# Reordering the gate pieces of the attention heads, and the opening's order, in a hybrid diffusion step

## The reference

```python
for l in range(DEPTH):
    ada = silu(c) @ w_ada[l] + b_ada[l]            # 9 vectors of 1024: shift, scale, gate
    h += 0.5 * g0 * swiglu(norm(h), ...)           # D_FF = 2816
    proj = n @ w_in[l]                             # hy, q_a, kv_a, k_r, fn, gates (3 x 1024)
    y_a = hyena(hy, filters(l))                    # two filters, made from a small sine MLP
    p = softmax(q @ k.T * scale); y_b = p @ v      # 8 heads, keys = latent + cached context
    y_c = real(fft2(fn))
    y = (sigmoid(ga)*y_a + sigmoid(gb)*y_b + sigmoid(gc)*y_c) @ w_out[l]
    h += g1 * y
    h += 0.5 * g2 * swiglu(norm(h), ...)
```

## Time and profile before

| | |
|---|---|
| median of three runs | 3245.68 us |
| profiled execution | 3245.85 us, span 3244.1 us |
| TensorE busy (matmul) | 3102.3 us, 96% |
| TensorE weight loads busy | 3025.4 us, 93% |
| VectorE busy | 1743.3 us, 54% |
| ScalarE busy | 966.7 us, 30% |
| mean granted clock of TensorE | 0.982 of full |

### The profile page before, as it was taken

One profiled execution on the slowest core, in us unless ns is written; L12 is line 12 of the kernel. 1 busy time (PEld: TensorE's weight loads), 2 busy tenths in 40 slices (PEclk: granted clock), 3 DMA queues, 4 the chain that ended last, 5 costly groups with the idle time before them and its releaser, 6 DMA issues.

```text
span 3244.1 us, 47824 instructions
## 1 busy us (share of the span) xinstructions
PE 3102.3 (96%) x20540; PEld 3025.4 (93%) x20540; DVE 1743.3 (54%) x2873; ACT 966.7 (30%) x1445; POOL 47.4 (1%) x92
## 2 busy tenths in 40 slices
PE   6899999988999999999999999999899999999998
PEld 3799999987899899999999999998789989999998
DVE  5655666556565565344465466565555545632334
ACT  2332322322444433122233121232244433322222
POOL 0000000000000000000000000000000000000000
PEclk8899999989999999999999999999999999999999
DMA  6145543456222523232223343335712252322221
GB/s 258 73 183 206 227 165 141 163 195 240 74 77 97 192 106 110 92 113 84 106 88 124 124 153 126 144 121 229 276 69 82 73 194 104 116 92 79 78 75 63
DMA packets 78933, 430.61 MB, mean 133 GB/s; under 512 B 8849, under 2 KB 12369, under 8 KB 46722
## 3 DMA queue, kind: packets, MB, share of 16 engines
q1 hardware_dynamic: 58656, 324.56, 27.1%
q0 software_dynamic: 9504, 56.78, 4.6%
q10 hardware_dynamic: 10562, 46.21, 3.6%
HBM read 370.73 MB, written 56.79 MB: 132 GB/s over the span
## 4 chain that ended last, share of the span: by engine, by line
PE 78%; DVE 11%; DMA 4%; ACT 4%; issue 3%; ACTq 0%; DVEq 0%; POOL 0%
PE tile_psum L568 37%; PE tile_psum L575 19%; PE tile_psum L919 4%; PE tile_psum L529 3%; PE tile_psum L494 2%; PE tile_psum L923 2%; PE misc_psum L494 2%; PE tile_psum L775 2%; PE tile_psum L534 1%; DVE wlo L1615 1%; PE tile_psum L703 1%; ACT whi L1160 1%; DMA raw<-in_w_proj 1%; DMA raw<-in_w_mix 1%; DVE h L1771 1%
## 5 line engine op out<-in xcount | busy, mean ns | idle before, releaser
L568 PE MATMUL tile_psum<-n_hi,whi 128*128 128x320 f32 x3264 | 744.3, 309 | 4.2 <-issue 2.2
L568 PE MATMUL tile_psum<-n_lo,whi 128*128 128x320 f32 x3264 | 742.3, 309 | 0.0
L568 PEld LDWEIGHTS tile_psum<-n_hi,whi 128*128 128x128 f32 x3264 | 546.4, 188 | 7.2 <-DVE n_lo L1693 4.6
L1615 DVE TENSOR_TENSOR wlo<-raw,whi 128x2048 fp32r<-128x2048 f32 (+2 forms) x202 | 443.5, 2196 | 193.5 <-ACT whi L1160 191.0
L568 PEld LDWEIGHTS tile_psum<-n_lo,whi 128*128 128x128 f32 x3264 | 546.9, 188 | 0.0
L575 PE MATMUL tile_psum<-n_hi,wlo 128*128 128x320 f32 x3264 | 512.1, 308 | 0.0
L575 PEld LDWEIGHTS tile_psum<-n_hi,wlo 128*128 128x128 f32 x3264 | 486.9, 188 | 0.0
L1160 ACT ACTIVATE whi<-raw 128x2048 fp32r<-128x2048 f32 (+2 forms) x202 | 369.9, 1831 | 373.9 <-DMA raw<-in_w_up 180.4
L568 PE MATMUL tile_psum<-x_hi,whi 128*128 128x320 f32 x1408 | 319.9, 308 | 0.0
L568 PE MATMUL tile_psum<-x_lo,whi 128*128 128x320 f32 x1408 | 319.7, 308 | 0.0
L1827 DVE TENSOR_TENSOR hidden<-gate_act,tile_psum 128x320 f32<-128x320 f32 x176 | 85.6, 487 | 375.3 <-ACT gate_act L1259 374.7
(11 more groups left out here) (285 smaller groups left out, 3601.3 us busy)
## 6 DMA issues: line engine op xcount, KB each, us to landing
raw<-in_w_up SPq DMA_DIRECT2D x88, 1024.0 KB, 4.8
w_ada<-in_w_ada SPq DMA_DIRECT2D x128, 512.0 KB, 5.7
raw<-in_w_down SPq DMA_DIRECT2D x32, 1024.0 KB, 4.8
raw<-in_w_gate SPq DMA_DIRECT2D x24, 1024.0 KB, 4.8
whi<-table_keep SPq DMA_DIRECT2D x20, 1024.0 KB, 4.8
wlo<-table_keep SPq DMA_DIRECT2D x20, 1024.0 KB, 7.4
g_keep<-gate_out POOLq DMA_DIRECT2D x48, 320.0 KB, 2.4
gates<-g_keep POOLq DMA_DIRECT2D x16, 960.0 KB, 6.8
```

Source lines behind the costliest of these rows:

```text
L568: pe.matmul(tps[:, t.s, m, 0:TH], blk(p, m * n + k)[0], (hi, lo)[b][:, k, tok], start=k == 0 and b == 0, stop=False)
L1615: dve.tensor_tensor(wlo[:, r, 0:cols], raw[:, r, 0:cols], whi[:, r, 0:cols].bitcast(F32), ALU.subtract)\
```

## The change

Two order lists are rewritten, one wait is moved, and `turn_signs(1)` is moved.

```diff
@@ head_order
-            order += [("S", n), ("F", 0)]
+            order += [("S", n)]
         if 1 <= n <= 5 * HEADS:
             order.append(("N", n - 1))
         if n >= 2:
-            order += [("T", n - 2)] + [("F", 0)] * (n != 2)
+            order += [("T", n - 2), ("F", 0), ("F", 0)]
...
-    order += [("F", 0)] * 2
+    order += [("F", 0)]
@@ first_order
-    beside = [[[("chain",)], at(0, "max") + [("add", 0)] + ada, ada * 2],
-              [ada * 2, [("add", 1)] + at(1, "max"), ada + [("add", 2)] + ada],
-              [ada * 2, [("add", 3)] + at(2, "max"), ada * 2]]
+    ahead = [[("chain",)] + ada * 2, ada * 4, ada * 4]
+    behind = [at(0, "max") + [("add", 0)], [("add", 1)] + at(1, "max") + [("add", 2)], [("add", 3)] + at(2, "max")]
     for n in range(3):
-        steps += [("square", (0, 1, 3)[n])] + at(n, "filter", 0) + beside[n][0] + taps(n + 1, 0, 2)
-        steps += [("round",)] * (n == 1) + [("small",)] * (n == 2)
-        steps += at(n, "filter", 1) + beside[n][1] + [("square", 2)] * (n == 1) + taps(n + 1, 2, 2)
-        steps += [("round",)] * (n == 2) + at(n, "filter", 4) + at(n, "norms") + beside[n][2] + taps(n + 1, 4, 1) + at(n + 1, "abs")
-    steps += [("sums",)] + at(3, "filter", 0) + ...
+        steps += [("square", (0, 1, 3)[n])] + ahead[n] + at(n, "filter", 0) + taps(n + 1, 0, 2)
+        steps += [("round",)] * (n == 1) + [("small",)] * (n == 2) + at(n, "filter", 1) + [("square", 2)] * (n == 1) + taps(n + 1, 2, 2)
+        steps += [("round",)] * (n == 2) + behind[n] + at(n, "filter", 4) + at(n, "norms") + taps(n + 1, 4, 1) + at(n + 1, "abs")
+    steps += [("sums",)] + ada + at(3, "filter", 0) + ...
@@ first_filter on TensorE
                     if l == o == 0:
                         pe.wait_ge(start_tables, due(start_tables, 32))
-                        pe.wait_ge(small_in, due(small_in, 16))
+                elif (l, o, f) == (0, 0, 4):
+                    pe.wait_ge(small_in, due(small_in, 16))
@@ first_taps on VectorE
                 if (l, o, t) == (1, 0, 0):
+                    turn_signs(1)
                     filter_hidden(1)
@@ first_chain on VectorE
-                turn_signs(1)
                 chain(2)
```

More of the change, by code:

```diff
@@ L199, in at @@
         return [(what, *orders[n], *which)]
-    beside = [[[("chain",)], at(0, "max") + [("add", 0)] + ada, ada * 2],
-              [ada * 2, [("add", 1)] + at(1, "max"), ada + [("add", 2)] + ada],
-              [ada * 2, [("add", 3)] + at(2, "max"), ada * 2]]
+    ahead = [[("chain",)] + ada * 2, ada * 4, ada * 4]
+    behind = [at(0, "max") + [("add", 0)], [("add", 1)] + at(1, "max") + [("add", 2)], [("add", 3)] + at(2, "max")]
     steps = taps(0, 0, 2) + taps(0, 2, 2) + taps(0, 4, 1) + at(0, "abs") + [("turned",)] + ada
     for n in range(3):
-        steps += [("square", (0, 1, 3)[n])] + at(n, "filter", 0) + beside[n][0] + taps(n + 1, 0, 2)
-        steps += [("round",)] * (n == 1) + [("small",)] * (n == 2)
-        steps += at(n, "filter", 1) + beside[n][1] + [("square", 2)] * (n == 1) + taps(n + 1, 2, 2)
-        steps += [("round",)] * (n == 2) + at(n, "filter", 4) + at(n, "norms") + beside[n][2] + taps(n + 1, 4, 1) + at(n + 1, "abs")
-    steps += [("sums",)] + at(3, "filter", 0) + at(3, "max") + [("spread", 0, 4)] + at(3, "filter", 1) + [("spread", 4, KT)]
+        steps += [("square", (0, 1, 3)[n])] + ahead[n] + at(n, "filter", 0) + taps(n + 1, 0, 2)
+        steps += [("round",)] * (n == 1) + [("small",)] * (n == 2) + at(n, "filter", 1) + [("square", 2)] * (n == 1) + taps(n + 1, 2, 2)
+        steps += [("round",)] * (n == 2) + behind[n] + at(n, "filter", 4) + at(n, "norms") + taps(n + 1, 4, 1) + at(n + 1, "abs")
+    steps += [("sums",)] + ada + at(3, "filter", 0) + at(3, "max") + [("spread", 0, 4)] + at(3, "filter", 1) + [("spread", 4, KT)]
     steps += at(3, "filter", 4) + at(3, "norms")
```

## The result

The changed kernel takes 3276.23 us (median of four runs, 3273.43 to 3280.64), the kernel before 3246.1 beside it: a ratio of 1.0093, 95% interval 1.0081 to 1.0105, so 30 us slower. The profiled execution spans 3271.6 us, before 3244.1.

A forecast was written before the change was run, and what follows sets the result against it. TensorE's order was taken to set the time, so new waits lengthen the kernel. Opening -10.8, heads +29.4 and half clock +5 sum to +23.6 on 3245.85: 3269 us, range 3246 to 3288.

The forecast's parts named there:

- Rival B: Opening brings next to nothing (crowded ada loads, filters starting at half clock), heads lose as forecast: 3277 us, chance 0.12.
- the heads' sum: Both heads stages: itemised gains and losses of 14.7 us a layer, +29.4 for two, before the half-clock allowance.
- Clock: Half clock behind the heads' new waits of about 2.5 us: +5 us, between 0 and 17.
- The opening: Opening: two long waits move behind ready work, so the first normalisation and FFN start earlier: -10.8 us, between -14 and -7.
- the clock's term: Opening: 1.1 us taken off the earlier start of abs, 11.9 us, for stretches at half clock.
- V0: Start of the heads stage: F5 and F6 come behind T0, idle time ahead of V0 grows to 6.5 us: +2.5 a layer.
- P0, P2 and V1: Heads: T follows P0 and P2 sooner, +0.9 each; at V1 T11 finds tile 0 full, +1.5 a layer.
- V2 and V3: Heads: panel parts delay tile 0, waits of 1.5 and 2.7 us at T21 and T22, likewise V3: +8.3 a layer.
- The new heads: At Q2, Q4 and Q6: delayed maximum, L9 and L13 delay the key's low part, old waits go: +3.2 a layer.
- The end: End of the heads stage: with two fills between T's the waits of 1.78 and 0.80 go: -2.6 a layer.
- an ordinary step: Heads: S, T, F, F instead of S, F, T, F, about 5.0 us a step, slack 1.4: gains and loses nothing.
- Rival A: Heads order costs nothing, if ScalarE gets T20's high part out before R10 matters: 3232 us, not slower, chance 0.15.

The follow-up runs named there:

- heads_only: The kernel before with the three changed lines of the head order alone, its opening untouched: 3279.8 us, ratio 1.0105 to before.
- opening_only: The changed kernel with the three head-order lines as before, so only the opening is changed: 3244.7 us, ratio 0.9998 to before.
- opening_warm2: opening_only plus idle matmuls nobody reads, 3, 4 and 6 ahead of the first three filters' norms, 4 ahead of layer 1's first taps: 3239.9 us, 0.9984.
- after_v0: The changed kernel with gate pieces F5 and F6 back ahead of V0, one fewer behind T4 and T24, panel parts shifting along: 3260.0 us, 1.0044.
- after_panels_late: The changed kernel with every panel part (R, L) that stands between scores and transposes moved behind that step's transposes: 3266.6 us, ratio 1.0064.
- after_v0_alone: The changed kernel with only F5 and F6 back ahead of V0, every other entry keeping its place: 3272.4 us, ratio 1.0083.
- opening_warm: opening_only plus idle matmuls nobody reads, 4, 8 and 8 ahead of the first three filters' norms, 12 ahead of layer 1's first taps: 3243.6 us, 0.9995.

## Why the prediction was right, and where not

It said 3269 and slower; it came to 3276.2, inside the range, slower by 30 and not 23.6 us. Rival B (the opening brings next to nothing, the heads lose as forecast: 3277) describes the outcome better than the forecast, though not by its reasons: VectorE shows no wait for an ada load, and the half clock that cost something fell on the norms and last taps. That the heads' sum fits is partly luck: `heads_only` measured +34.4, the forecast's 29.4 + 5, out of two errors of opposite sign (under Clock, below).

- **The opening, -10.8: mis-sized.** `opening_only` measured -0.7 us, within -3.6 to +2.3. The chain through VectorE was right: with the norms and last taps at full clock (`opening_warm2`) abs began at 98.41 and the first normalisation at 106.84, at the times forecast, and the FFN 12.1 us earlier than before. In part that is luck: the third filter began at 75.71 there, 2.4 us ahead of the 78.1 laid out, and its round took as much longer. The step that failed is the clock's term, "I take off 1.1 for stretches at half clock", with the 2.4, 2.9 and 3.9 us for norms and last taps. From the norms' start to the next filter's first piece (the third time to abs) the forecast has 4.1, 4.6 and 3.9 us, where the addition on VectorE is counted in the first two; the changed kernel took 6.5, 6.5 and 6.8. That is 7.2 of the 8.2 us by which abs came late (106.60 against 98.4). A wait moved ahead of the norms puts the half clock on the norms and the last taps, for which VectorE waits three times in a row. The Trainium skill (TensorE: Matmul & The Clock Gate, Part 1) has the half rate follow idling and full rate return after sustained work; the trace agrees: the windows above have 0.50 to 0.51 behind each of the four waits, and the piece at 89.48, between two of the stretches, is back at 3.62 us.
- **V0, +2.5: right in its wait** (6.5 forecast, 6.50 measured), short in its price. P0 came 3.21 us later into the stage with one piece fewer ahead of it, so 4.97 at equal pieces. The excess fits the half clock, 13.65 us that begin 4.8 us before the wait ends.
- **P0, P2 and V1** (0.9, 0.9, 1.5): right. The waits of T5, T15 and T11 are 0.78, 0.78 and 1.25.
- **V2 and V3, +4.2 each**: T21 and T22 wait 1.29 and 2.14, not 1.5 and 2.7. With half clock the stretches from P3 to P4 and P5 to P6 are 5.3 and 3.8 us longer. The order on the engines (R10 ahead of T20's high part, L11 ahead of T21's low part) is in the rows. But the two waits don't belong one to each part. With R10 and L10 earlier T22's wait is gone, even where L11 still stands ahead of T21's low part (`after_v0`), and T21's 1.24 stays. With R10 and L11 moved behind T20 and T21 (`after_panels_late`) T21's wait is gone and T22's is 1.76.
- **The new heads, +3.2**: S20 and S30 wait 2.13 and 2.12 behind L9 and L13, as written out. T9's 2.4 was 0.67. Unforeseen are T8, T18 and T28 (1.52, 0.89, 1.52): they share tile 0 with the query of the new head, which VectorE is still rotating (q_f, until 872.7); before, a piece stood between. No run puts one back there. The stretches from P0 to P1, P2 to P3 and P4 to P5 grew by 1.6, 3.0 and 1.9 us, where 1.5, 2.2 and 1.3 were forecast with P0's and P2's own.
- **The end, -2.6**: -2.9 (P6 to P7, at equal pieces).
- **Clock, +5**: too small. Waits grew by 10.9 us in layer 0 (14.7 forecast), and half clock cost the other 8.2 (2.5 forecast). Two errors of opposite sign leave 19.1 there, and 16.5 in layer 1, against 17.2 a layer. On the waits the forecast left out what also went: F48's 1.30 and the 0.44 ahead of P1, P3 and P5.
- **The Trainium skill's rule on rotating PSUM banks** (Perfetto Trace Analysis, Matmuls) was set aside for an ordinary step, and rightly: no ordinary T waits. The waits come where a transposition follows closely on another use of the same tile: T8, T18 and T28 behind a query, T5 and T15 (0.78) behind a product.
- **Rival A** (ScalarE gets past R10) is refuted by R10's row at 965.97, behind which T20's high part starts at 967.77. Its time was also added up wrong: an end of 2.6 a layer gives 3246 - 11 - 5 = 3230, not 3232.

The profiled spans add up: 5.3 us earlier at the first heads stage (2.95 of it from the opening), 19.1 more in it, 2.3 less up to the second, 16.5 more in that, 0.5 less to the end: +27.5. The 2.4, 2.3 and 0.5 outside opening and heads no experiment assigns.

## What to carry to other kernels

Price a wait with what runs right behind it: half clock on a large product costs little if the product has slack, but on small work that another engine is waiting for it ate an opening's whole gain. When filling work moves in a list in which other work is placed by counting, follow each displaced entry to its queue: here the waits that we put down to panel parts (S20, S30, T11, T21, T22, T31, T32) are 12.0 of the 22.3 us of new waits in layer 0, and parts moved by hand cost as much when they came early, ahead of their own transfer. The best version left the order of the other entries alone and moved one piece from the end, where it covered nothing, to the longest wait; most of its gain came from what that shifted elsewhere.

## What had not been expected of the hardware

Waits far below V0's were followed by half clock, but the length of one wait does not decide it. In the changed kernel those of 2.13 and 2.14 us at S20 and T22 were (0.51 and 0.52 in the windows), and T32's, also 2.14, was not. T8's 1.52 was not in the changed kernel, and in `after_v0_alone` the same wait of 1.52 was, with half clock from 870.53 on for 3.41 us. A 128x512 fp32 matmul takes 0.86 to 0.87 us (twelve in 10.46), so idle work can be matched to a wait only in steps of that size; in `opening_warm` the surplus cost what the clock gave.
